# Early adaLN jobs of a hybrid SSD/gMLP step: the weights' rows as products, or their columns

## The reference, cut to what matters

```python
silu_c = jax.nn.silu(c)
silu_cctx = jax.nn.silu(c_ctx)[None, :]
for i in range(DEPTH):                                  # DEPTH = 2
    mod_ctx = silu_cctx @ w_ada[i] + b_ada[i]           # w_ada[i] is 1024 x 3072
    mod_lat = silu_c @ w_ada[i] + b_ada[i]
    h_ctx, st = _layer(h_ctx, mod_ctx, h0_ctx, lw, None)
    h_lat, _ = _layer(h_lat, mod_lat, state_ssm[:, i], lw, rows if i % 2 == 1 else None)
def _layer(x, mod, h0, lw, rows):
    shift, scale, gate = jnp.split(mod, 3, axis=-1)
    h = rms_norm(x, norm_w) * (1 + scale[:, None]) + shift[:, None]
    proj = h @ w_in
    ...   # SSD branch and gMLP branch, two output projections, merge
    return x + gate[:, None] * (merged @ w_out), h_fin
```

## Time and profile before

| | us |
|---|---|
| median of three runs | 1401.3 |
| the profiled execution's own time | 1401.26 |
| its span, first to last instruction | 1399.5 |
| PE busy | 1387.0 (99%) |
| DVE busy | 1027.1 (73%) |
| POOL busy | 1029.1 (74%) |
| ACT busy | 467.1 (33%) |

### The profile page before, as it was taken

How to read it: one execution, slowest core, us unless ns; L and a number is a source line. 1 busy time by engine, 2 the same in 40 slices (tenths; PEclk the granted TensorE clock), 3 DMA queues, 4 the chain that set the end, 5 groups by cost and what they waited for, 6 DMA issues and landing times.

```text
span 1399.5 us, 27040 instructions
## 1 busy us (share of the span) xinstructions
PE 1387.0 (99%) x10101; PEld 1331.1 (95%) x10101; DVE 1027.1 (73%) x1503; ACT 467.1 (33%) x1039; POOL 1029.1 (74%) x1421
## 2 busy tenths in 40 slices
PE   8999999999999999999999999999999999999997
PEld 5899999999999999999998999999999999999997
DVE  6988679665677688999978766976566776869234
ACT  5432123214766333001252323241266661320122
POOL 3789886696554499998869898657765546979763
PEclk9999999999999999999999999999999999999999
DMA  9362665123766555444334455722346665453222
GB/s 366 126 151 76 191 167 159 61 66 127 188 179 192 177 204 212 150 151 155 106 136 122 107 165 149 192 86 61 106 135 191 193 173 201 139 190 120 76 76 91
DMA packets 198047, 206.85 MB, mean 148 GB/s; under 512 B 76592, under 2 KB 163760, under 8 KB 196784
## 3 DMA queue, kind: packets, MB, share of 16 engines
q1 hardware_dynamic: 116000, 155.13, 35.6%
q10 hardware_dynamic: 81936, 50.16, 12.4%
HBM read 179.23 MB, written 26.02 MB: 147 GB/s over the span
## 4 chain that ended last, share of the span: by engine, by line
PE 98%; DVE 1%; DMA 0%; SPq 0%; issue 0%; ACT 0%; DVEq 0%; ACTq 0%
PE acc L718 79%; PE X L684 5%; PE acc L684 3%; PE X L972 2%; PE X L952 2%; PE X L988 1%; PE X L1013 1%; PE acc L866 1%; PE X L981 1%; DVE p_lo L1606 1%; DMA ada_pre<-in_wada 0%; DVE ssq L1581 0%; PE X L825 0%; DVE xr L2143 0%; PE X L910 0%; PE acc L732 0%
## 5 line engine op out<-in xcount | busy, mean ns | idle before, releaser
L617 POOL CAST w_hi<-w_st 128x256 fp32r<-128x256 f32 x696 | 410.5, 604 | 337.1 <-PE acc L718 162.2
L621 POOL TENSOR_TENSOR w_lo<-w_st,w_hi 128x256 fp32r<-128x256 f32 x696 | 645.0, 936 | 0.0
L718 PE MATMUL acc<-h_hi,w_hi 128*128 128x320 f32 x1696 | 402.1, 318 | 0.0
L718 PE MATMUL acc<-h_lo,w_hi 128*128 128x320 f32 x1696 | 386.3, 309 | 0.0
L718 PE MATMUL acc<-h_hi,w_lo 128*128 128x320 f32 x1696 | 386.2, 309 | 0.0
L718 PEld LDWEIGHTS acc<-h_hi,w_hi 128*128 128x128 f32 x1696 | 284.4, 188 | 14.7 <-issue 11.8
L718 PEld LDWEIGHTS acc<-h_hi,w_lo 128*128 128x128 f32 x1696 | 283.5, 188 | 0.0
L718 PEld LDWEIGHTS acc<-h_lo,w_hi 128*128 128x128 f32 x1696 | 283.4, 188 | 0.0
L1824 DVE SCALAR_TENSOR_TENSOR cv<-raw,convw_sb,cv 128x642 f32<-128x642 f32 x128 | 137.2, 1072 | 4.5
L1540 DVE SCALAR_TENSOR_TENSOR ada_acc<-ada_st,sc,ada_acc 128x512 f32<-128x512 f32 x112 | 107.8, 1002 | 1.8
L1280 ACT ACTIVATE cvt<-cv 128x642 f32<-128x642 f32 x32 | 23.8, 744 | 158.1 <-DVE cv L1824 158.1
(11 more groups left out here) (264 smaller groups left out, 2322.5 us busy)
## 6 DMA issues: line engine op xcount, KB each, us to landing
w_st<-in_wts SPq DMA_DIRECT2D x174, 512.0 KB, 3.7
cum_bc<-cum_dram ACTq DMA_DIRECT2D x80, 256.0 KB, 5.0
ada_st<-in_wada SPq DMA_DIRECT2D x34, 512.0 KB, 4.3
ex_bc<-ex_dram ACTq DMA_DIRECT2D x64, 128.0 KB, 3.1
ada_pre<-in_wada SPq DMA_DIRECT2D x14, 512.0 KB, 8.9
xs<-xs_dram SPq DMA_DIRECT2D x64, 80.0 KB, 3.8
mga_dram<-c_buf SPq DMA_DIRECT2D x16, 320.0 KB, 5.2
xf<-xf_dram SPq DMA_DIRECT2D x4, 1280.0 KB, 7.1
```

The lines of the kernel that those rows point to most:

```text
L617: nc.gpsimd.tensor_copy(quarter(w_hi, slot, q), quarter(w_st, slot, q)).then_inc(s_pool, 1)
L621: nc.gpsimd.tensor_tensor(quarter(w_lo, slot, q), quarter(w_st, slot, q), f(quarter(w_hi, slot, q)), ALU.subtract).then_inc(w_split, 1)
L718: last = mm(a[:, hf, 0:n1], w[:, s, cols], x[:, k, hf * HALF:hf * HALF + n1], start=(k == 0 and n == 0), stop=(k == KC - 1 and n == 2))
```

## The change

Jobs 0 to 3 are made another way. `job_piece(n, i)` takes piece i of job n as soon as that piece is there: blocks of 32 columns of the weights are the stationary operand, and the two columns of the conditioning (`sc`) move. Each piece is 2 x 4 x 4 = 32 matmuls of two columns, a job 128, and the result stands in X[2] as columns, added up over k in PSUM; each job has 8 columns of its own there. `first_mm`, `row_copy`, `first_tp`, `scp` and `ada_row` go away.

The order is changed with it. On PE, job 1's pieces stand between the first chunks, `dt_part(0, 0)` moves behind chunk 5 of tile 1, `stat_mm` behind chunk 7 of tile 0, `stat_bc` behind chunk 6 of tile 1, and job 3's pieces are four hooks in tile 2. On ACT, `first_p` goes ahead of the squares for chunks 4 to 7. On DVE, `job_out(1)` stands behind two squares in place of five, and `dt_scaled` is one call. On SP the weights of dt are loaded behind the last piece of x.

```diff
@@ SP
-                sp.dma_start(ada_first(n), wada[L, q, hf, n % 4, :, :, :]).then_inc(pre_in[n // 2], 16)
+                sp.dma_start(ada_first(n), wada[L, q, hf, n % 4, :, :, :]).then_inc(pre_in[n], 16)
...
-        dt_weight(0)
         half_weight(0, 1)
         half_weight(1, 1)
         first_x(3)
+        dt_weight(0)
         first_ada(2)
...
-        sp.wait_ge(row_mm, 2)
+        sp.wait_ge(ada_mm, 2)
@@ PE
-            chunks((1, 0), (1, 1), (0, 2))
-            first_mm(1)
-            chunks((1, 2))
-            first_tp(1)
-            chunks((0, 3), (1, 3))
-            dt_part(0, 0)
-            keep_pace(1, X[0])
-            chunks((0, 4), (0, 5), (1, 4))
+            chunks((1, 0))
+            job_piece(1, 0)
+            chunks((1, 1))
+            job_piece(1, 1)
+            chunks((0, 2))
+            job_piece(1, 2)
+            job_piece(1, 3)
+            chunks((1, 2), (0, 3), (1, 3))
+            chunks((0, 4), (0, 5), (1, 4), (1, 5))
             pe.wait_ge(x_in, 16)
-            dt_part(0, 1)
-            stat_mm(0)
-            first_mm(2, range(DTG))
-            stat_bc(0)
+            for half in range(2):
+                dt_part(0, half)
+            job_piece(2, 0)
             chunks((0, 6))
             chunks((0, 7)).then_inc(tile_done, 1)
-            first_mm(2, range(DTG, KC))
-            chunks((1, 5))
-            first_tp(2)
+            stat_mm(0)
+            job_piece(2, 1)
             chunks((1, 6))
+            stat_bc(0)
+            job_piece(2, 2)
+            job_piece(2, 3)
             chunks((1, 7)).then_inc(tile_done, 1)
...
-                 hooks=[(2, lambda: first_mm(3)), (4, lambda: first_tp(3)), (6, first_shifts), (8, last_shifts)])
+                 hooks=[(1, lambda: job_piece(3, 0)), (2, lambda: job_piece(3, 1)), (3, lambda: job_piece(3, 2)),
+                        (4, lambda: job_piece(3, 3)), (5, first_shifts), (8, last_shifts)])
...
+        def job_piece(n, i):
+            if n == 0 and i == 0:
+                pe.wait_ge(sc_ready, 1)
+            if i == 0 and n > 0:
+                pe.wait_ge(job_read, n)
+            pe.wait_ge(pre_in[4 * n + i], 16)
+            w = ada_first(4 * n + i)
+            for e in range(2):
+                k = 2 * i + e
+                for j in range(4):
+                    for b in range(4):
+                        last = mm(job_sums(n)[32 * b:32 * b + 32, :, j], tokens(w[:, e, :], j, b), sc[:, 1, k, :],
+                                  start=(k == 0 and j == 0), stop=(k == KC - 1 and j == 3))
+            if i == 3:
+                last.then_inc(ada_mm, 1)
...
         keep_pace(4)
-        first_mm(0, range(DTG))
-        keep_pace(1)
-        first_mm(0, range(DTG, KC))
-        keep_pace(2)
-        first_tp(0)
-        keep_pace(4)
+        for i in range(3):
+            job_piece(0, i)
+            keep_pace(1)
+        job_piece(0, 3)
+        keep_pace(6)
@@ ACT
-        row_copy(0)
...
-        square(0, 4, xr[:, 4, :])
-        row_copy(1)
-        square(0, 5, xr[:, 5, :])
         first_p(4)
         first_p(5)
+        square(0, 4, xr[:, 4, :])
+        square(0, 5, xr[:, 5, :])
         act.wait_ge(x_in, 16)
+        first_p(6)
+        first_p(7)
         square(0, 6, xr[:, 6, :])
         square(0, 7, xr[:, 7, :])
-        first_p(6)
-        first_p(7)
         root(0)
         rs_copy(0)
-        row_copy(2)
@@ DVE
-        for k in range(KC // 2):
-            add_square(0, k)
...
-        add_square(0, 4)
-        dt_scaled(0, 0, DTG)
+        add_square(0, 0)
+        add_square(0, 1)
         job_out(1)
-        add_square(0, 5)
-        first_low(4)
-        first_low(5)
-        dt_scaled(0, DTG, KC)
-        add_square(0, 6)
-        add_square(0, 7)
-        first_low(6)
+        add_square(0, 2)
+        add_square(0, 3)
+        for k in (4, 5):
+            first_low(k)
+        for k in (4, 5):
+            add_square(0, k)
+        dt_scaled(0, 0, KC)
+        for k in (6, 7):
+            first_low(k)
+        for k in (6, 7):
+            add_square(0, k)
         rstd(0)
-        first_low(7)
```

More of the change, by code:

```diff
@@ L260, in build @@
     xo = place("xo", [P, 2, PITCH], r_t + 20 * PITCH)
-    scp = place("scp", [P, KC, 32], r_t + 20 * PITCH)
     dts = place("dts", [P, KC, 2, 32], r_t + 28 * PITCH)
@@ L292, in build @@
     r_a0, r_a1 = region(4096), region(4096)
-    ada_row = place("ada_row", [P, 2, 512], r_a1)
     ada_acc = [place(f"ada_acc{i}", [P, 2, 512], at) for i, at in enumerate((r_a0, r_a1))]
@@ L352, in build @@
     ada_used, ada_mm = sem("ada_used"), sem("ada_mm")
-    pre_in = [sem(f"pre_in{i}") for i in range(2 * NF)]
-    row_mm, row_out, job_read = sem("row_mm"), sem("row_out"), sem("job_read")
+    pre_in = [sem(f"pre_in{i}") for i in range(4 * NF)]
+    job_read = sem("job_read")
     c_in, ct_ready, sc_ready = sem("c_in"), sem("ct_ready"), sem("sc_ready")
@@ L394, in ada_first, with job_sums @@
         return ada_pre[n][:, :, :] if n < len(ada_pre) else ada_st[:, n - len(ada_pre), :, :]
-    def job_rows(n):
-        return acc[0][:, 0, :] if n == 0 else X[2][:, :]
+    def job_sums(n):
+        at = 8 * n if n < NF else 0
+        return X[2][:, at:at + 8].rearrange("p (v j) -> p v j", v=2)
     DT_FIRST = (X[3][:, 0:HALF], X[1][:, 0:HALF], X[1][:, HALF:HALF + 2])
@@ L805, in job_mm @@
             for b in range(4):
-                last = mm(X[2][32 * b:32 * b + 32, 0:8].rearrange("p (v j) -> p v j", v=2), sel[:, :], sums[:, b, :, :],
+                last = mm(job_sums(NF)[32 * b:32 * b + 32, :, :], sel[:, :], sums[:, b, :, :],
                           start=True, stop=True)
@@ L1137, in _ @@
         warm_root()
[L1138 to L1143, removed]
         def first_p(k):
@@ L1207, in _ @@
                 act.wait_ge(job_read, 3)
[L1208 to L1211, removed]
+                for k in range(KC):
                     if k == KC // 2:
@@ L1565, in job_out @@
             cols = slice(4 * hf, 4 * hf + 4)
-            total = X[2][:, 0:8].rearrange("p (v j) -> p v j", v=2)
-            TT(mods[:, 3 * L + q, :, cols], total,
+            TT(mods[:, 3 * L + q, :, cols], job_sums(n),
                bada_sb[:, 3 * L + q, cols].unsqueeze(1).broadcast_to([P, 2, 4]), ALU.add).then_inc(job_read, 1)
@@ L1596, in _ @@
             own.mark(nc.vector.memset(dtb_sb[at:2 * at, :], 0.0))
-        own.mark(nc.vector.memset(scp[:, :, :], 0.0))
         dve.wait_ge(ct_ready, 1)
         own.link(STT(out=sc[:, 1, :, :], in0=sc[:, 0, :, :], scalar=1.0, in1=c_sb[:, :, :], op0=ALU.add, op1=ALU.mult))
-        own.link(TS(sc[:, 1, :, :], sc[:, 1, :, :], 0.5, None, ALU.mult))
-        nc.vector.tensor_copy(scp[:, :, 0:2], sc[:, 1, :, :]).then_inc(sc_ready, 1)
+        TS(sc[:, 1, :, :], sc[:, 1, :, :], 0.5, None, ALU.mult).then_inc(sc_ready, 1)
         def first_low(k):
```

## The result

The changed kernel takes 1423.2 us, median of five runs (1421.7 to 1424.2), against 1401.2: a ratio of 1.0156, 95% interval 1.0145 to 1.0167. The forecast was 1405.2, at most 1408. The direction was right and the size far off. The changed kernel also scatters over 2.5 us, the one before over 0.5.

The account below looks back on a forecast made before the run. PE was taken as the bound over the long middle, with DVE setting the opening's pace until 28.6 us; start, to tile 2, tile 2 and hrows summed to +3.95 us on 1401.26, giving 1405.2, 8-in-10 range 1401.6 to 1408.

Parts of the forecast that it names:

- The order's part: Opening: 15 chunks instead of 11 ahead of stat_bc, so tile 2 waits for unscaled(0) and starts 2.8 us later.
- start: Opening up to chunk (1,0): it starts at 16.5 us instead of 16.64, a gain of 0.15.
- to tile 2: From chunk (1,0) to the start of tile 2: later stat_bc and a wait on PE, 2.95 us lost.
- tile 2: Within tile 2: four lone pieces take 3.38 us instead of 2.62, plus a 0.1 wait for job_out(2); 0.85 in all.
- hrows: Behind tile 3's start: DVE ends hrows late, a second PE wait of 0 to 1.2 us, taken as 0.3.
- Unit prices: New products on PE: 0.085 + 0.0086 us a record, about 0.2 more between chunks; a lone piece there costs 0.84.
- Job 0: Opening: pieces and three keep_pace end at 10.75 us, bias read at 10.9, 0.9 earlier; first chunk at 13.4.
- POOL's gate: Chunk (1,0) waits for tile 1's first low part, which POOL ends at 16.4 us, so an earlier first chunk gains little.
- To stat_bc: PE's list from chunk (1,0) to stat_bc, forecast to stand at 37.7 us instead of 32.49, 5.2 later.
- the idle time on p_lo: Ahead of stat_bc: PE idles about 1.4 us in chunks (0,4) and (0,5), then waits 0.35 for DVE.
- The wait for unscaled(0): Start of tile 2: PE comes at 40.4 us, DVE's accumulator ends at 42.0, a new wait of 1.6.
- B: Rival, opening: narrow products and gaps drop TensorE to 1.2 GHz, 4 us at half rate at the start; 1408.7, chance 0.08.

Follow-up runs that it names:

- narrow_sparse: Kernel before plus extra narrow products far behind the opening: 32 records behind 24 chunks, 64 behind every second chunk (12 places), 128 once; 1426.6 us.
- half_products: Changed kernel with every second chunk k left out of the sums of jobs 0 to 3, so 32 records a piece, not 64; 1411.6 us.
- rows_new_order: Kernel before with the changed kernel's order on PE, ACT, DVE and SP, all four jobs still rows; 1408.9 us.
- cols_old_order: Kernel before in its own order, jobs 1 to 3 in columns where the rows' products stood, job 0 as rows; 1420.8 us.
- job0_cols: Kernel before with job 0 alone made in columns, jobs 1 to 3 still rows, all orders as before; 1406.1 us.
- job0_rows: Changed kernel with job 0 alone made as rows again, with the old start of PE's list; 1418.5 us.
- job3_sparse: Kernel before with job 3 alone in columns, 64 records behind tile 2's first chunk, 32 behind each of six more, job_out(3) later on DVE; 1409.4 us.

## Why the forecast was wrong

The forecast's sum was -0.15 (start) + 2.95 (to tile 2) + 0.85 (tile 2) + 0.3 (hrows). Measured by the same marks it is 4.3 + 7.8 + 7.7 + 0.5 = 20.4. The order's part was a right mechanism mis-sized; the terms for job 0 and tile 2 counted the new products' time and left out two things that the runs show: stalls of PE while its next instructions are fetched, and a lower clock behind them.

**Unit prices: right.** 0.0086 us a record and 0.2 to 0.3 a place gave 25 us for narrow_sparse, which took 25.4. The 25 ns of the Trainium skill (TensorE: Matmul & The Clock Gate, Back-to-back issue gap) were rightly refused for this kind of product: a piece alone costs 10 ns a record in the change as well.

**Job 0: wrong, and this is the first failed step.** "Four pieces (2.54), three keep_pace of 0.43" took work for time. It took 7.9 us in place of 4.2, 6.9 to 14.8, with 0.96 a piece, 1.15 a keep_pace and a stall of 0.4; the six keep_pace behind took 4.2 in place of 2.6. The first chunk came 5.6 us later than forecast and (1,0) 4.5: POOL's gate, which I had trusted to swallow a gain, hid 1.1 of a loss. That half_products finds the gate just where I had it says that this step failed by PE's pace alone.

**To stat_bc: the order was right, the sum wrong.** The forecast 5.2 became 14.0. Of the 8.8 missed, 4.5 were there at (1,0); from there on stalls of 2.5 and 0.9 and 6.8 us at half speed (3.4) make 6.8, and the idle time on p_lo that I had counted (1.4 and 0.35) fell away, since PE was late itself. That makes 5.0 for the 4.3 that are left; the rest of 0.7 is in small terms that I had put too high.

**The wait for unscaled(0): right mechanism.** It is in the change (0.41, the rest of it taken up by a stall of 1.3 ahead; tile 2 starts 4.9 us behind stat_bc, where I had 4.3), and by itself in rows_new_order (2.4). My argument had DVE as never idle from stat_bc on; before, it waits 0.6 us for ACT's copy just behind stat_bc, and only from there on it is never idle. Rows in the new order cost 7.8, of which I had 3: the waits were under-read by 1.4 and each drew 3.4 us at the lower level behind it, which costs 1.7.

**Tile 2: mis-sized worst.** "Four pieces alone, 3.38" was right as work. Tile 2 took 19.8, not 12.9: nearly all of it at the lower level, 2.86 for a chunk and a piece in place of 1.73.

**hrows** was no issue: DVE was done with them at 73.15, and PE came for them at 77.1.

**The rivals.** B had the lower clock, but a single time at the start and by gaps or width; it got 0.08 and 1408.7. B's mechanism, the lower clock, is thus part of the truth, in three stretches and not one, and its price was still 14.5 us short. That the direction of my own forecast came out was no luck, since the order that it rested on costs 7.8 by itself; but most of the loss came by ways that I did not have. What none of mine had is the supply of instructions. The rows could have hinted at it: I counted the new products' time and never their number, 3 jobs of 256 records where rows and turns are 48, and the page of the profile lists the instruction queue.

The loss thus divides, as far as runs show it: order 7.8 and start 5.0, each alone; the form of jobs 1 to 3 on top of the order 9.6. Together 22.4, near the 22.0, though cols_old_order shows that these parts don't add up in general.

## What to carry to other kernels

Count instructions, not only time: a rewrite that replaces a few wide products by many narrow ones must leave PE enough wide work that the next block of 256 instructions arrives, here 2.2 to 2.9 us. No run here shows a spacing that does it in this opening; 64 records to two chunks did it in the middle of the kernel, but for one stall of 0.3. And price a wait of PE of some 2 us in a dense opening at about double, since what stands behind it ran at the lower clock in every such case here. Where a step shortens latency by taking engines out of a chain, first look whether something else (here POOL's split at 16.4) sets the time anyway.

## What was not expected of the hardware

PE stood still for 0.3 to 4.7 us within streams that wait for nothing, with a 16 KB packet on the instruction queue beside it, in a quiet part of the kernel (593.7 us, 7 GB/s) as in the loaded opening. Three stretches of the changed opening ran at half speed, and the profile's own clock column did not show the first of them. Chunks mixed with 64 records each stayed at the lower level for 32.5 us behind one stall of 1.6, while a thinner mix never left the upper one, and one with 32 records a chunk came back to it after 3.4 us. And a start with the same instructions on PE's list rose to the upper level at 7 us in job0_cols and only at about 18 in the changed kernel. Why is not known. In job0_rows, half_products and job3_sparse, which scatter over 3 to 9 us, the longer executions are those with the lower granted clock; so the time at the lower level differs from one execution to the next. What sets it was not tested.
